# Four stretches reordered: the delta rule's next low part, GpSimd's gate products, the experts' end, the sparse attention

## The chip, the cores and the metric

One core of a Trainium2 chip runs the whole program. The metric is the device time of one execution in microseconds, the median of several runs.

## The reference

Two blocks run in a row on x of 256 x 1024 in float32. The first: a mixer with a chunked gated delta rule and an mLSTM, a cross-attention to a memory, and an expert layer (PEER), then a norm. The second: a gated feed-forward (SwiGLU), a spatial gating, a sparse attention and more SwiGLUs, each with a layer norm. What matters here, cut:

```python
# delta rule, per chunk of 64
decay = jnp.exp(jnp.where(causal, gc[..., :, None] - gc[..., None, :], -jnp.inf))
a = jnp.where(strict, jnp.einsum('nbhid,nbhjd->nbhij', kb, k) * decay, 0.0)
t_inv = lax.linalg.triangular_solve(a + eye, ...)
...
go = rmsnorm(go.transpose(0, 2, 1, 3), gdn_norm_w) * jax.nn.silu(g_z...)
...
# sparse attention: per head three softmaxes of one query
s_c = jnp.einsum('bqghd,bngd->bghqn', q_b, k_cmp) + head_bias(dist_c)   # 15 compressed keys
p_c = masked_softmax(s_c, mask_c)          # a masked entry gives 0
o_s = ... selected keys ...                # all 256 keys, causal
o_w = ... window keys ...                  # all 256 keys, causal
return g_b[..., 0:1] * o_c + g_b[..., 1:2] * o_s + g_b[..., 2:3] * o_w
...
return out @ w_o
```

## The kernel before

Every weight comes through a ring of three slots in on-chip memory (1 MB each, `Weights`, filled by SyncE's DMAs at L179 as slots are used). A float32 matrix product is made of three passes of TensorE over split operands: ScalarE writes a slot's high part in two halves of 128 x 1024 (L247, or L301 where a stage begins one slot ahead), VectorE the low part, slot minus high (L256 or L307), and TensorE multiplies high by high, high by low and low by high (L398 to L400). A slot so split is ready when VectorE has signalled `used`. The order of the work on each engine is written out by hand, and the engines meet at semaphores. A stage is a block that all five engines enter and leave together, unless stages are joined. `stand_in` (L584) issues matmuls whose result nothing reads.

- **Delta rule, `gdn_prepare` (L1250 to L1450).** The 64 x 64 triangular matrices are inverted by doubling in six levels, each in two halves of the pairs (head, tile). VectorE picks a level's entries (`pick`, L1316) and subtracts products from `inv_T` (L1336) and `inv` (L1339). TensorE makes the products (L1426, L1431, L1435), and ScalarE copies between them (L1374). Beside it the first slot of the next stage is split ahead into `x_transposed`: ScalarE the high halves at steps 3 and 5 (L1377), GpSimd the low halves (L1390).
- **Recurrences, `memory_and_recurrences` (L1453 to L1856).** TensorE mixes eight panels of the memory's keys and values (`panel(f, j)`, L398 to L400) with the chunk steps `delta(n)`, `state_product(n)` and `memory_cell(n)`. VectorE makes the panels' low parts between the steps (`low(f)`, L256). ScalarE copies the chunk results out (`delta_out(n)`, which signals `rd`). GpSimd multiplies `kw` by its weights (L1851), the gates z and mo by the head gains (L1854, L1855), and then issues the DMA that writes the position bias of 4 MB (L1856). The gates are read at the stage's end.
- **Experts' end (L2400 to L2620).** After the last expert's product of a row tile VectorE adds the tile (`add(t)`, L2602), ScalarE squares it with the sum and takes the root (L2429, L2432), VectorE scales it (`scale(t)`, L2610) and TensorE transposes tile 0 (L575), with stand-ins before and after. ScalarE (`begin.highs`, L301) and VectorE (`begin.low`, L307) split the next stage's first slot as well.
- **Sparse attention, `query_and_attend` (L3605 to L3935), then `out_and_norm` (L2763).** Eight pairs of heads. Per pair VectorE adds the bias to the scores (L3818, L3819, L3822) and takes three negated maxima (L3827, L3830, L3833), and between these does the last steps of the pair before: mask, sum, guard, reciprocal, gate, weigh (L3775 to L3802). ScalarE takes eight exponentials with a sum (L3881) and four small ones for the compressed keys (L3887), and copies the transposed probabilities of each head out in three pieces (L3897 to L3899). TensorE, in iteration n: scores of pair n, transposes of the even head of pair n-2 (`turn`, L3708 to L3712), `mix` of pair n-3 (L3726), transposes of the odd head. ScalarE's order in iteration n is below. In the last three iterations TensorE makes stand-ins. Then `out_and_norm` multiplies by w_o in four slots (24 matmuls of 128x512 each), the first split at the attention's end.

```python
            for n in range(NH // 2 + 3):
                if 2 <= n < NH // 2 + 2:
                    copy(2 * (n - 2))
                    copy(2 * (n - 2) + 1)
                if n < NH // 2:
                    exps(n)
```

## Time and profile before

| | |
|---|---|
| median of 3 runs | 2301.25 us (2296.02 to 2301.57) |
| profiled execution, its time | 2301.07 us |
| profiled execution, its span | 2299.0 us |
| granted TensorE clock, mean | 0.989 of full speed |
| TensorE busy | 2221.3 us (97%) |
| VectorE busy | 1591.0 us (69%) |
| ScalarE busy | 1176.1 us (51%) |
| GpSimd busy | 44.3 us (2%) |

The profile shows one execution. Times in it count from the span's start. Engines are PE (TensorE), PEld (its weight loads), DVE (VectorE), ACT (ScalarE), POOL (GpSimd) and SP (SyncE). L12 is line 12 of the kernel. A timeline's row has start (us), length (us), engine, line, operation and tiles. A float32 matmul outside the split products appears as two records. "[1.24 <-ACT ...]" gives the idle time before a row and what ended it. [...]

### The profile page before, as it was taken

What the parts mean: (1) busy time and instruction counts of PE and PEld (TensorE: products, weight loads), DVE (VectorE), ACT (ScalarE), POOL (GpSimd) and SP (SyncE); (2) the same over time, 40 slices, a digit from 0 to 9 for tenths busy, and PEclk for the clock granted to TensorE, in tenths of its full rate; (3) what the DMA queues carried; (4) which work ended last, traced back from release to release, by engine and by line L of the source; (5) the groups of instructions that cost most, each with busy time, mean ns of one, the idle gap of its engine ahead of it and who ended that gap; (6) DMA issues with size and microseconds to landing.
All of it is one profiled execution on the core that took longest, in us unless ns stands there. A gap on an engine that the chain in (4) does not pass through costs nothing. (4 is left out here: it accounts for less than half of the span.)

```text
span 2299.0 us, 37165 instructions
## 1 busy us (share of the span) xinstructions
PE 2221.3 (97%) x14670; PEld 1983.5 (86%) x14670; DVE 1591.0 (69%) x2807; ACT 1176.1 (51%) x2063; POOL 44.3 (2%) x23
## 2 busy tenths in 40 slices
PE   8889999999999999999999999999999999989998
PEld 8877789899999988888888889988888788868887
DVE  7866658999889976666666656766556555676555
ACT  6532444455554445565555545445443544585444
POOL 0111000100000000000000000000000000000000
PEclk9989999999999999999999999999999999999999
DMA  7407534455444446666646456545555655404552
GB/s 267 147 13 147 178 129 149 153 178 176 147 147 147 147 148 193 193 195 195 193 166 222 184 197 235 188 149 202 198 183 204 221 201 183 151 2 165 201 193 99
DMA packets 78309, 389.97 MB, mean 170 GB/s; under 512 B 9771, under 2 KB 12715, under 8 KB 49868
## 3 DMA queue, kind: packets, MB, share of 16 engines
q1 hardware_dynamic: 76684, 383.33, 47.9%
q0 software_dynamic: 1040, 4.19, 1.5%
q8 instruction: 106, 1.74, 0.3%
q10 hardware_dynamic: 432, 0.33, 0.1%
q14 instruction: 47, 0.39, 0.0%
HBM read 382.57 MB, written 5.24 MB: 169 GB/s over the span
## 5 line engine op out<-in xcount | busy, mean ns | idle before, releaser
L256 DVE TENSOR_TENSOR split_slots<-ring,split_slots 128x1024 fp32r<-128x1024 f32 x402 | 480.0, 1239 | 136.4 <-ACT split_slots L247 136.0
L247 ACT ACTIVATE split_slots<-ring 128x1024 fp32r<-128x1024 f32 x402 | 402.3, 1054 | 159.3 <-PE banks L400 138.6
L409 DVE SCALAR_TENSOR_TENSOR expert_lo<-ring,expert_hi 128x512 fp32r<-128x512 f32 x512 | 362.5, 713 | 170.6 <-ACT expert_hi L404 169.5
L3025 PE MATMUL banks<-x_transposed,split_slots 128*128 128x512 f32 x1360 | 478.3, 395 | 2.0 <-PEq L464 2.0
L404 ACT ACTIVATE expert_hi<-ring 128x512 fp32r<-128x512 f32 x512 | 323.9, 633 | 264.2 <-PE banks L400 264.2
L3026 PE MATMUL banks<-x_transposed,split_slots 128*128 128x256 f32 x1360 | 381.6, 281 | 0.0
L3025 PEld LDWEIGHTS banks<-x_transposed,split_slots 128*128 128x128 f32 x1360 | 255.4, 188 | 62.1 <-issue 2.2
L398 PE MATMUL banks<-x_transposed,expert_hi 128*128 128x256 f32 x1024 | 295.3, 288 | 6.6 <-DVE expert_lo L409 6.6
L399 PE MATMUL banks<-x_transposed,expert_hi 128*128 128x256 f32 x1024 | 289.0, 282 | 0.0
L400 PE MATMUL banks<-x_transposed,expert_lo 128*128 128x256 f32 x1024 | 289.0, 282 | 0.0
L3026 PEld LDWEIGHTS banks<-x_transposed,split_slots 128*128 128x128 f32 x1360 | 256.4, 189 | 1.5
L398 PE MATMUL banks<-expert_hi,weighted_split 128*128 128x512 f32 x512 | 200.1, 391 | 3.1 <-issue 3.1
L398 PEld LDWEIGHTS banks<-x_transposed,expert_hi 128*128 128x128 f32 x1024 | 194.5, 190 | 8.1 <-issue 4.4
L3125 DVE TENSOR_TENSOR gate_and_value<-banks,products_with_low_parts 128x512 f32<-128x512 f32 x88 | 60.8, 691 | 201.8 <-ACT products_with_low_parts L3081 201.8
L399 PE MATMUL banks<-expert_lo,weighted_split 128*128 128x512 f32 x512 | 199.8, 390 | 0.0
L400 PE MATMUL banks<-expert_hi,weighted_split 128*128 128x512 f32 x512 | 199.7, 390 | 0.0
L399 PEld LDWEIGHTS banks<-x_transposed,expert_hi 128*128 128x128 f32 x1024 | 194.4, 190 | 0.0
L400 PEld LDWEIGHTS banks<-x_transposed,expert_lo 128*128 128x128 f32 x1024 | 194.3, 190 | 0.0
L3081 ACT ACTIVATE products_with_low_parts<-banks 128x512 f32<-128x512 f32 x88 | 52.6, 597 | 245.2 <-PE banks L3026 237.4
L398 PE MATMUL banks<-x_transposed,split_slots 128*128 128x256 f32 x544 | 154.8, 285 | 2.3 <-PEq L464 2.0
L400 PE MATMUL banks<-x_transposed,split_slots 128*128 128x256 f32 x544 | 153.5, 282 | 0.0
L399 PE MATMUL banks<-x_transposed,split_slots 128*128 128x256 f32 x544 | 153.4, 282 | 0.0
(494 smaller groups left out, 4088.1 us busy)
## 6 DMA issues: line engine op xcount, KB each, us to landing
ring<-in_ffn_w SPq DMA_DIRECT2D x132, 1024.0 KB, 4.8
ring<-in_peer_u SPq DMA_DIRECT2D x128, 512.0 KB, 3.5
ring<-in_peer_v SPq DMA_DIRECT2D x128, 512.0 KB, 3.6
ring<-in_w_in SPq DMA_DIRECT2D x16, 1024.0 KB, 4.9
ring<-in_sgu_w_in SPq DMA_DIRECT2D x16, 1024.0 KB, 4.9
ring<-in_peer_wq SPq DMA_DIRECT2D x8, 1024.0 KB, 6.1
ring<-in_sgu_w_out SPq DMA_DIRECT2D x8, 1024.0 KB, 4.7
ring<-in_kv_w SPq DMA_DIRECT2D x6, 1024.0 KB, 4.8
```

The costliest lines, as they stand in the source:

```text
L247: act.activation(self.parts[:, b, 0, p], self.k.w.slot(g)[:, p], ACT.Copy).then_inc(self.high_done, 1)
L256: ins = dve.tensor_tensor(self.parts[:, b, 1, p], self.k.w.slot(g)[:, p], self.parts[:, b, 0, p].bitcast(F32), ALU.subtract)
L398: pe.matmul(out, lh, rh, start=start, stop=False)
L399: pe.matmul(out, lh, rl, start=False, stop=False)
L400: return pe.matmul(out, ll, rh, start=False, stop=stop)
L404: return act.activation(dst, src, ACT.Copy, scale=scale)
L409: return dve.scalar_tensor_tensor(dst, src, scale, hi.bitcast(F32), ALU.mult, ALU.subtract)
L3025: pe.matmul(out(j, slice(0, 2 * SEQ)), lh, k.xT.both[:, c, :, :], start=(c == 0), stop=False)
L3026: ins = pe.matmul(out(j), ll, rh, start=False, stop=(c == DC - 1))
L3081: act.activation(rest[:, n, :, :], sums(u, n, 1), ACT.Copy).then_inc(copied[n], 1)
L3125: dve.tensor_tensor(whole[:, n, :, :], sums(u, n, 0), rest[:, n, :, :], ALU.add).then_inc(joined[n], 1)
```

## The change

1. In the delta rule ScalarE makes the first high half at the stage's start and the second at step 3. VectorE makes the low halves, one before its wait for the decays and one before its wait for `w_done`. GpSimd does none of it.
2. In the recurrences GpSimd issues the bias DMA before the two gate products, and these wait for `rd` to reach 3, the third chunk's `delta_out`.
3. At the experts' end ScalarE makes each high half after the square and root of a tile, not both before; VectorE makes the first low half after `scale(0)`, not after `add(0)`.
4. In the attention the mask is a product of 16 gate columns, made once; the guard goes; the compressed scores get their negated maximum added on VectorE (`shift`), and one exponential replaces four. One copy of 128x1024 replaces three. ScalarE puts the second tile's exponentials between the two copies. The first slot of w_o is split during the attention and multiplied there: tile 0 in iteration 8, tile 1 in iteration 9, in place of the stand-ins. `out_and_norm` starts at its second slot, which is split at the attention's end.

```diff
         @block.vector
         def _(dve):
             link = linker(dve, vs)
+
+            def ahead_low(n):
+                dve.wait_ge(ahead_high, n + 1)
+                return dve.tensor_tensor(ahead_parts[1][n], ahead_slot[n], ahead_parts[0][n].bitcast(F32), ALU.subtract)
+
...
             link(dve.tensor_tensor(col[:, 3, :], s.run[:, 0, 1, :], gc, ALU.subtract))
+            ahead_low(0)
             dve.wait_ge(ps, 1)
...
+            ahead_low(1).then_inc(k.w.used[ahead % RING], 1)
             dve.wait_ge(w_done, 1)
...
+            act.wait_ge(k.w.loaded[ahead % RING], 16 * (ahead // RING + 1))
+            ahead_high_of(0)
             act.activation(col[:, 1, :], gc, ACT.Exp).then_inc(acts, 1)
...
+                if n == 3:
+                    ahead_high_of(1)
...
             k.sig.clear_other(pool)
-            for n in range(2):
-                pool.wait_ge(ahead_high, n + 1)
-                ins = pool.tensor_tensor(ahead_parts[1][n], ahead_slot[n], ahead_parts[0][n].bitcast(F32), ALU.subtract)
-            ins.then_inc(k.w.used[ahead % RING], 1)
...
+            pool.dma_start(k.a["bias_rows"].rearrange("p h x -> h p x"),
+                           bias.rows[:, :].unsqueeze(1).broadcast_to([NH, P, DISTS])).then_inc(k.bias_stored, 16)
             pool.wait_ge(landed, 32)
+            pool.wait_ge(rd, 3)
...
             act.wait_ge(w_low, KEYS)
-            begin.highs(act)
...
+                begin.high(act, t)
...
             add(0)
-            begin.low(dve, 0)
             add(1)
             dve.wait_ge(gain_landed, 16)
             scale(0)
+            begin.low(dve, 0)
             scale(1)
...
+        def output_product(pe, i):
+
+            if i == 0:
+                pe.wait_ge(biased, 3 * NH // 2)
+                pe.wait_ge(written, 2)
+                rows.ready(pe, 0)
+            wh, wl = rows.rows(0)
+            for r in range(2):
+                ins = down_tile(pe, k, k.xT.at(slice(0, P), r), (wh[:, r, :], wl[:, r, :]), i, r == 0, False)
+            if i == 1:
+                ins.then_inc(rows.eaten, 1)
...
                 if n == NH // 2:
-                    pe.wait_ge(biased, 3 * NH // 2)
-                    stand_in(pe, k, 6)
-                if n == NH // 2 + 1:
-                    stand_in(pe, k, 4)
-                    pe.wait_ge(expd, NH // 2)
-                    stand_in(pe, k, 12)
+                    output_product(pe, 0)
...
+                if n == NH // 2 + 1:
+                    output_product(pe, 1)
+                if n == NH // 2 + 2:
+                    mix(pe, n - 3)
...
+                    if n == 2:
+                        rows.low(dve, 0)
...
+            rows.low(dve, 1)
             for j in range(NH // 2 - 3, NH // 2):
                 output(j)
...
+        def mask_gates(dve):
+
+            own = gates[:, :, :].rearrange("p i (h n) -> p i h n", n=3)[:, 0, :, 0]
+            dve.wait_ge(narrow_read, 2)
+            dve.tensor_tensor(own, own, masks[:, 0, 0:1].broadcast_to([P, NH]), ALU.mult).then_inc(gates_masked, 1)
...
+        def shift(dve, q):
             own = cs[q % 3][:, :, :, 0:NCMP]
+            dve.wait_ge(negmax, 3 * q + 3)
+            dve.tensor_tensor(own, own, spread(c[q % 3][:, 0, :, :, 0], NCMP), ALU.add).then_inc(shifted, 1)
...
+            def cmp_exps(q):
+                own = cs[q % 3][:, :, :, 0:NCMP]
+                act.wait_ge(shifted, q + 1)
+                act.activation(own, own, ACT.Exp).then_inc(expd, 1)
...
-                act.activation(pT[b][:, :, :, :].rearrange("p a i n -> p (a i n)"), k.psum[:, 4, :], ACT.Copy).then_inc(copied, 1)
-                act.activation(flat(pT_last[b][:, :, :]), k.psum[:, 5, 0:B], ACT.Copy).then_inc(copied, 1)
-                act.activation(cT[b][0:NCMP, :], k.psum[0:NCMP, 5, B:2 * B], ACT.Copy).then_inc(copied, 1)
+                act.activation(turned_T[b][:, :, :].rearrange("p a n -> p (a n)"),
+                               k.psum[:, 4:6, :].rearrange("p b n -> p (b n)"), ACT.Copy).then_inc(copied, 1)
...
                 if 2 <= n < NH // 2 + 2:
                     copy(2 * (n - 2))
+                if n < NH // 2:
+                    exps(n, 1)
+                if 2 <= n < NH // 2 + 2:
                     copy(2 * (n - 2) + 1)
                 if n < NH // 2:
-                    exps(n)
+                    exps(n, 0)
+                    cmp_exps(n)
```

VectorE's instructions at the start of the delta rule, before:

```order
L1297 TENSOR_TENSOR gc_diagonal<-constants_sb,running_logs 128x512
L1299 COPY gdn_columns<-beta 128x8
L1301 TENSOR_TENSOR gdn_columns<-running_logs 128x8
L1303 TENSOR_TENSOR decay_up<-banks,running_logs 128x512
L1304 SCALAR_TENSOR_TENSOR decay_low<-decay_up,constants_sb 128x512
```

and now:

```order
L1302 TENSOR_TENSOR gc_diagonal<-constants_sb,running_logs 128x512
L1304 COPY gdn_columns<-beta 128x8
L1306 TENSOR_TENSOR gdn_columns<-running_logs 128x8
L1300 TENSOR_TENSOR x_transposed<-ring,x_transposed 128x4x256
L1309 TENSOR_TENSOR decay_up<-banks,running_logs 128x512
L1310 SCALAR_TENSOR_TENSOR decay_low<-decay_up,constants_sb 128x512
```

The first low half stands ahead of `decay_up`, for which VectorE waits on TensorE.

ScalarE's instructions of one pair in the middle of the attention, before:

```order
L3897 ACTIVATE probabilities_T<-banks 128x512
L3898 ACTIVATE probabilities_last_T<-banks 128x256
L3899 ACTIVATE cmp_probabilities_T<-banks 15x256
L3881 ACTIVATE scores_second,softmax_columns<-scores_second,softmax_columns 128x256 x4
L3881 ACTIVATE scores_first,softmax_columns<-scores_first,softmax_columns 128x128 x4
L3887 ACTIVATE cmp_scores<-cmp_scores,softmax_columns 128x15 x4
L404 ACTIVATE x_transposed<-banks 128x256
```

(the three copies stand there twice, for the even and the odd head), and now:

```order
L3917 ACTIVATE probabilities_T<-banks 128x1024
L3903 ACTIVATE scores_second,softmax_columns<-scores_second,softmax_columns 128x256 x4
L3917 ACTIVATE probabilities_T<-banks 128x1024
L3903 ACTIVATE scores_first,softmax_columns<-scores_first,softmax_columns 128x128 x4
L3910 ACTIVATE cmp_scores<-cmp_scores 128x4x15
L404 ACTIVATE x_transposed<-banks 128x256
```

The larger exponentials stand between the two heads' copies.

VectorE at the experts' end, now (before, the first L307 row stood between the two adds):

```order
L2610 TENSOR_TENSOR x_natural<-banks,x_natural 128x1024 x2
L2614 RECIPROCAL final_stats<-final_stats 128x1
L2618 SCALAR_TENSOR_TENSOR x_natural<-x_natural,final_stats,final_gain 128x512 x2
L307 TENSOR_TENSOR split_slots<-ring,split_slots 128x1024
L2614 RECIPROCAL final_stats<-final_stats 128x1
L2618 SCALAR_TENSOR_TENSOR x_natural<-x_natural,final_stats,final_gain 128x512 x2
L307 TENSOR_TENSOR split_slots<-ring,split_slots 128x1024
```

Both adds stand together, and each scaling is followed by a low half.

## Rows read from the trace of the kernel before

**Rows 1.** VectorE, delta rule: timeline; L1316's own (ns min/median/max).
```profile
134.88 0.69 DVE L1303 TENSOR_TENSOR decay_up<-banks,running_logs 128x512 f32<-128x512 f32 x1 [1.48 <-PE banks L1396]
...
L1316 DVE TENSOR_TENSOR A_level<-A,constants_sb x12: 411/418/2471, 138.3 to 157.5; 128x256 f32<-128x256 f32 x12
...
147.81 2.47 DVE L1316 TENSOR_TENSOR A_level<-A,constants_sb 128x256 f32<-128x256 f32 x1
...
165.39 1.22 DVE L1352 COPY w_T<-banks 128x1024 f32<-128x1024 f32 x1 [1.39 <-PE banks L1446]
```

**Rows 2.** Timeline of GpSimd, delta rule and recurrences.
```profile
147.66 2.34 POOL L1390 TENSOR_TENSOR x_transposed<-ring,x_transposed 128x1024 fp32r<-128x1024 f32 x1 [0.71 <-ACT x_transposed L1377]
...
188.49 3.33 POOL L1855 TENSOR_TENSOR mlstm_o<-mlstm_o,head_gains 128x1024 f32<-128x1024 f32 x1
```

**Rows 3.** Timeline of TensorE, delta rule.
```profile
142.80 0.66 PE L1431 MATMUL banks<-AtW,inv 64*64 64x64 f32 x16
...
151.09 1.12 PE L1426 MATMUL banks<-inv_T,A_level 64*64 64x64 f32 x16 [2.37 <-DVE inv L1339]
...
156.00 0.66 PE L1431 MATMUL banks<-AtW,inv 64*64 64x64 f32 x16
...
159.22 1.35 PE L1431 MATMUL banks<-AtW,inv 64*64 64x64 f32 x32
```

**Rows 4.** Timelines of VectorE and TensorE, recurrences.
```profile
186.24 6.66 DVE L256 TENSOR_TENSOR split_slots<-ring,split_slots 128x1024 fp32r<-128x1024 f32 x2
...
193.04 0.55 PE L398 MATMUL banks<-memory_T,split_slots 128*128 128x256 f32 x1 [2.85 <-DVE split_slots L256]
```

**Rows 5.** Windows: stretch, length, busy us (instructions) of PE to POOL, clock, DMA.
```profile
167.00:171.00 4.00, 4.00 (x21) 4.00 (x22) 1.87 (x4) 1.91 (x2) 1.41 (x2) 0.57 0.18 51
...
193.00:198.10 5.10, 5.06 (x24) 5.09 (x24) 4.95 (x6) 1.22 (x2) 0.00 (x0) 0.50 0.85 92
...
2044.00:2062.00 18.00, 13.37 (x133) 10.39 (x132) 15.26 (x35) 15.51 (x64) 0.00 (x0) 1.00 0.01 1
```

**Rows 6.** Timelines of ScalarE, TensorE and VectorE, experts' end.
```profile
1197.38 2.01 ACT L301 ACTIVATE split_slots<-ring 128x1024 fp32r<-128x1024 f32 x2 [5.27 <-DMA ring<-in_ffn_w]
...
1196.50 0.40 PE L400 MATMUL banks<-expert_hi,weighted_split 128*128 128x512 f32 x1
...
1202.58 1.42 DVE L2610 SCALAR_TENSOR_TENSOR x_natural<-x_natural,final_stats,final_gain 128x512 f32<-128x512 f32 x2
...
1203.91 1.22 DVE L307 TENSOR_TENSOR split_slots<-ring,split_slots 128x1024 fp32r<-128x1024 f32 x1
...
1206.65 1.07 PE L575 MATMUL banks<-ident,x_natural 128*128 128x128 f32 x8 [0.30 <-PEq L479]
```

**Rows 7.** Timelines, attention; the last row groups lines by form.
```profile
1998.42 1.23 DVE L3818 TENSOR_TENSOR scores_second<-banks,position_bias 128x1024 f32<-128x1024 f32 x1 [1.29 <-PE banks L3696]
...
2045.55 1.21 DVE L3818 TENSOR_TENSOR scores_second<-banks,position_bias 128x1024 f32<-128x1024 f32 x1
...
2047.69 0.88 ACT L3887 ACTIVATE cmp_scores<-cmp_scores,softmax_columns 128x15 f32<-128x15 f32 x4
...
2048.61 0.22 DVE L3775 TENSOR_TENSOR cmp_scores<-cmp_scores,cmp_masks 128x60 f32<-128x60 f32 x1 [1.04 <-ACT cmp_scores L3887]
...
2051.09 0.60 ACT L3897 ACTIVATE probabilities_T<-banks 128x512 f32<-128x512 f32 x1 [1.25 <-PE banks L3712]
...
2053.46 1.21 DVE L3818 TENSOR_TENSOR scores_second<-banks,position_bias 128x1024 f32<-128x1024 f32 x1
...
2066.74 3.74 PE L584 MATMUL banks<-ones,ident 128*128 128x128 f32 x32
...
2078.74 0.50 PE L398 MATMUL banks<-split_slots,x_transposed 128*128 128x512 f32 x1
...
L3881 ACT ACTIVATE scores_second<-scores_second,softmax_columns 128x256 f32<-128x256 f32 x32 | 15.8, 494 | 6.3 <-DVE softmax_columns L3827 6.3
```

**Rows 8.** Windows, the attention's output stage, columns as in rows 5.
```profile
2079.00:2101.00 22.00, 22.00 (x95) 17.66 (x95) 14.03 (x16) 11.22 (x14) 0.00 (x0) 1.00 0.36 143
```

110 lines of the change are left out of this document (48 added, 62 removed).

## The prediction

> **What bounds the kernel.** I read the page first: TensorE is busy 97% of the span, so time can only leave where TensorE waits, works for nothing, or runs at the lower clock. So I read the four changed stretches one by one: timelines of VectorE, GpSimd and TensorE, then windows for the granted clock.
>
> In the delta rule's inversion VectorE's 12 picks (L1316) take 0.418 us in the median, but one takes 2.47 [rows 1]. It lies under a GpSimd subtraction that runs from 147.66 to 150.00 [rows 2]. TensorE then idles 2.37 us, and its next group takes 1.12 where a group takes 0.66 [rows 3]. In the recurrences two halves of a low part take 6.66 us together [rows 4] where one alone takes 1.22 [rows 6]; they end 1.08 us after the GpSimd product that starts at 188.49 and takes 3.33 [rows 2]. [...] At the experts' end ScalarE waits 5.27 us for a weight slot before it may square the rows [rows 6]. In the attention a pair of heads takes 7.91 us (2045.55 to 2053.46), of which VectorE idles 1.04 for ScalarE's small exponentials and ScalarE idles 1.25 between its two copies for TensorE's transposes [rows 7]. So the pairs are paced by ScalarE's 6.66 us plus one uncovered wait.
>
> **The sum, part by part** (against the profiled execution's 2301.07 us; the median of the runs, 2301.25, is the same for this purpose).
>
> *A. Delta rule: 3.5 us gained.* An undisturbed level takes 159.22 - 156.00 = 3.22 us. From 142.80 four levels would end at 155.68, not 159.22 [rows 3]: 3.54. Added to VectorE are two halves of 1.22 [rows 6]. The first falls into an idle of 1.48 us before L1303, the second into one of 1.39 before L1352 [rows 1]; I cost both at nothing. With that cover gone they would cost up to 2.4, so A lies between 1.1 and 3.9. ScalarE's first half, about 1.0 us (half of L301's 2.01 [rows 6]), now stands before its exponentials; VectorE's wait for them comes later, and if it did not hide, it would cost that 1.0, which the lower bound covers.
>
> What the row shows is a two-operand VectorE operation held until GpSimd's is over. [...]
>
> *B. Recurrences: 5.3 us gained.* Gone are the wait of 2.85 [rows 4] and the half clock behind it: 5.10 us at 0.50 would be 2.55 [rows 5]. I take 2.85 + 2.5. The two products (3.33 for the longer [rows 2]) now start after the third chunk's delta has been read. There they run beside the low part of panel 5. They can hold it 2 to 3.3 us, but TensorE has another panel and a chunk to do before it needs that part; I cost it at nothing, and at 3.3 at worst. The bias DMA now stands ahead of the products on GpSimd's queue. It starts some 6 us sooner and could slow a weight load. A panel's slot is asked for two panels before its use, so that too is nothing. B is 2 to 5.4.
>
> *C. Experts' end: 1.2 us gained.* ScalarE now squares tile 0 before it waits for the slot. The last product starts at 1196.50 and takes 0.40 [rows 6]. From 1197.0 VectorE is then busy without a break: the add of tile 1 (as long as a half, 1.14 to the next start), two scalings of 1.55 (the 1.42 pair and its reciprocal), two low halves of 1.14 and 1.22 [rows 6]. That ends at 1203.6. Now the stage ends when TensorE's stand-ins do, 0.30 before 1206.65 [rows 6], so 2.75 is won. But TensorE would be done near 1202.3 and idle 1.6 us before the next stage. At the block start at 167 such an idle is followed by 4.00 us at 0.57 [rows 5], a loss of 1.7. I take 1.5 off; the ends are 0 and 2.75.
>
> *D. Attention: 13.4 us gained*, in three terms.
> D1, the pairs. VectorE's own work is 7.91 - 1.04 = 6.87 a pair [rows 7]. The mask and guard go (some 0.2 of issue), the shift comes (0.15): 6.8. ScalarE's falls from 6.66 to about 6.1, since four small exponentials (0.88 [rows 7]) become one (0.3), and its idle of 1.25 is now filled by four exponentials of 0.49 [rows 7]. VectorE becomes the pace. Seven steps lead from pair 0 (1998.42) to pair 7 (2053.46): 55.04 us [rows 7]. After: the first stays at the mean 7.9 (it waits for the gate columns), six take 6.8, one of them carries the two halves of row 0's low part (2.3), and one waits about 0.5 for the last query products: 51.5. D1 = 3.5, between 0 (ScalarE still paces) and 5.
> D2, the tail from pair 7's start to the end of the last mix, now 2078.74 - 2053.46 = 25.3, with 32 stand-in passes of 3.74 us in it that delay a transpose [rows 7]. After, I walk the chain, with pieces of the same work as in rows 7 or estimated from it: pair 7's adds and first maximum 3.2; the second half's exponentials 2.0; the copy between 1.0; the first half's 1.55; the one small one 0.3; sum, reciprocal, gate and weighing 2.8; a wait for the copy of head 13, 1.1; transposes, mix and copy of head 14, 3.2; head 15's transposes 0.9; half of the moved product 2.8; the last mix 2.1. That is 21.0: D2 = 4.3, between 2 and 5.5.
> D3, the moved product: 24 of the output's 96 matmuls, 22.00 us for 95 recorded [rows 8], 0.232 each, leave the output stage: 5.6. Their first half falls where TensorE waited for VectorE, the second is counted in D2. Behind them the next slot must be split in time: row slot 2 is ready some 5.0 us after the last mix (ScalarE's last output and two halves, then VectorE's two) and wanted 5.6 after it, when slot 1's 24 matmuls are done. A miss costs under 1.
>
> Together 3.5 + 5.3 + 1.2 + 13.4 = 23.4, and 2301.07 - 23.4 = **2277.7 us**.
>
> [...] In the rows the clock stays at 1.00 from 2044 to 2062, where TensorE is busy only 13.37 of 18 us [rows 5], and the new tail is denser. [...]
>
> **The rivals.**
> R1, ScalarE still paces the pairs (a 128x1024 copy dearer than the three it replaces, or the copies still found waiting): D1 is 0, D2 halves to 2.1, the gain 17.7, so 2283.4. For it: ScalarE ends the waits today. Against: its work falls below VectorE's. Chance 0.12.
> R2, the clock falls in the attention's tail: the 8.7 us of TensorE's work from head 14's transposes to the last mix take twice as long: gain 23.4 - 8.7 = 14.7, so 2286.4. Chance 0.07.
> R3, the change only moves the hold: VectorE's stalls were hidden or come back at another step, and A and B are nothing: 23.4 - 8.8 = 14.6 is left, 2286.5. The waits in rows 3 and 4 speak against it. Chance 0.05.
> R4, slower. In the new order ScalarE's copy of an odd head stands behind exponentials that wait for VectorE's maximum of a later pair, which waits for TensorE's scores, which stand behind transposes that wait for such a copy. Round the ring: 3.2 + 2.0 + 1.0 + 0.9 + 2.1 + 0.9 + 1.9 and 0.4 of waits = 12.4 us. As I read the order it closes only after two pairs, 6.2 a pair, under the 6.8. If it closed in one, seven steps would take 86.8 instead of 55.0: 31.8 lost against 23.4 - 3.5 = 19.9 won elsewhere, 2313.0. It decides the sign from 10.7 us a pair. Chance 0.03.
> The forecast has 0.73.
>
> **How the numbers follow.** 2277.7 is the likeliest case. All parts at their best give 3.9 + 5.4 + 2.75 + 16.1 = 28.2, 2273; with a microsecond of spread between executions on either side of that and of R1 the range is 2272 to 2285; what lies above is R2, R3 and R4, 0.15, and some of R1's spread. About 0.3%, 6.9 us, is what a measurement of this kernel can tell. Everything but R4 is faster by more: 0.95; within 0.3% I leave 0.02 for losses that add up; slower 0.03.
>
> **What would show it.** A: no pick over 0.5 us, levels 3.2 apart. B: the low part of panel 2 in 2.4 us, TensorE's wait gone, clock 1.00 behind it; a held L256 near panel 5 with nobody waiting. C: squares right after the first add, the stage ended by VectorE, a low clock at the next start. D: pairs 6.8 apart, VectorE without idle, no wait between ScalarE's copies, the last mix some 8 us sooner. Pairs at 7.9 would make D1 wrong, a clock under 1.00 in the tail D2, an idle before row slot 2 D3.

## The result and the profile after

The changed kernel takes 2271.39 us in the median of 4 runs (2269.86 to 2275.18), the kernel before 2300.57 (2296.02 to 2301.57): ratio 0.9886, 95% interval 0.9872 to 0.9900. That is 29.2 us, more than the forecast's 23.4, and the median lies 0.6 us below the range's low end. The profiled execution took 2271.95 us, its span is 2269.8.

Both kernels were timed twice more. The medians differ by 25.5 us (2298.21 and 2272.69) and by 26.0 (2298.39 and 2272.36). So some 26 us is the change, and the rest of the first 29 is the scatter of single executions. Where the gain stands in the two profiles is found by pairing the same instruction in both traces and watching how far apart its two starts are:

| stretch | change's part | forecast | seen |
|---|---|---|---|
| start to the delta rule (code unchanged) | none | 0 | 4.4 |
| delta rule | A | 3.5 | 3.6 |
| recurrences | B | 5.3 | 5.3 |
| cross-attention to the experts' last product (unchanged) | none | 0 | 1.3 |
| experts' end | C | 1.2 | 2.9 |
| SwiGLU to the attention (unchanged) | none | 0 | -2.1 |
| attention and its output | D | 13.4 | 14.0 |

The parts sum to 25.7, the unchanged stretches to 3.6 (sums of unrounded figures). The -2.1 is mostly clock too: the changed kernel's profile has a granted clock of 0.80 over 1529 to 1536, where the same work ran at 1.00 before, and 1.5 us are lost there.

**The unchanged start.** TensorE's first products in the timelines, of the kernel before and then of the changed one (start, length):

```profile
20.57 0.40 PE L359 MATMUL banks<-x_transposed,split_slots 128*128 128x256 f32 x1
20.78 0.30 PE L356 MATMUL banks<-x_transposed,split_slots 128*128 128x256 f32 x1
```

```profile
14.69 0.39 PE L356 MATMUL banks<-x_transposed,split_slots 128*128 128x256 f32 x1 [2.32 <-DVE split_slots L307]
14.92 0.28 PE L359 MATMUL banks<-x_transposed,split_slots 128*128 128x256 f32 x1
15.04 0.28 PE L356 MATMUL banks<-x_transposed,split_slots 128*128 128x256 f32 x1
```

The same matmul starts 0.21 us apart at first and 0.12 later, the spacings that these 128x256 products have elsewhere at a granted clock of 0.50 (24 in 5.10 us [rows 5]) and of 1.00 (0.12 apart from 1190.80 on in the changed kernel). Before, the higher level came at 20.8, in the changed kernel's profile at 14.9; it is read from the spacing alone, since the windows show 1.00 over 13 to 21 in both profiles. That is worth 2.7 us by 43. The other 1.7 come in the window 60 to 90, where the granted clock is 0.94 before and 1.00 in the changed kernel. In the 14 profiles of this case (all have this stretch unchanged up to the first mixer panels) the first rise came between 14.8 and 20.8. The start of the delta rule (the product `gc_diagonal`) lies at 132.31 before and at 127.89 after, and in the eleven others that leave all ahead of it alone between 127.85 and 132.11. An early rise alone does not give an early start: in e6 it came at 14.9, but the clock was low again later (products 0.21 us apart from 15.9 to 19.1, 0.94 over 60 to 90), and the delta rule began at 131.05. So the 4.4 us are the placing of the low clock, not the change.

**A and B.** The picks in the changed kernel (the tile's own view: count, ns min/median/max, first and last start), then the timelines of VectorE and GpSimd in the recurrences:

```profile
L1322 DVE TENSOR_TENSOR A_level<-A,constants_sb x12: 417/420/425, 133.9 to 149.5; 128x256 f32<-128x256 f32 x12
```

```profile
178.26 2.35 DVE L256 TENSOR_TENSOR split_slots<-ring,split_slots 128x1024 fp32r<-128x1024 f32 x2
...
204.26 2.92 DVE L256 TENSOR_TENSOR split_slots<-ring,split_slots 128x1024 fp32r<-128x1024 f32 x2
207.11 0.68 DVE L1647 TENSOR_TENSOR mlstm_state<-mlstm_state,chunk_decays 128x516 f32<-128x516 f32 x1
210.53 0.69 DVE L1682 TENSOR_TENSOR mlstm_state<-mlstm_state,banks 128x516 f32<-128x516 f32 x1 [2.74 <-PE banks L1595]
...
200.24 2.38 POOL L1864 TENSOR_TENSOR gdn_z<-gdn_z,head_gains 128x1024 f32<-128x1024 f32 x1 [21.28 <-ACT convolved_T L1789]
202.59 2.37 POOL L1865 TENSOR_TENSOR mlstm_o<-mlstm_o,head_gains 128x1024 f32<-128x1024 f32 x1
```

No pick is over 0.43 us [rows 1 had 2.47]. In the kernel before a second pick was held as well, and behind both TensorE ran at half clock (timeline of VectorE, then window):

```profile
145.31 1.92 DVE L1316 TENSOR_TENSOR A_level<-A,constants_sb 128x256 f32<-128x256 f32 x1
```

```profile
150.00:154.00 4.00, 2.92 (x56) 2.94 (x58) 1.75 (x6) 0.38 (x1) 0.00 (x0) 0.57 0.01 4
```

By the paired starts 2.3 of A's 3.6 us are the two holds and 1.2 the half clock behind them.

In the recurrences the picture is as forecast. The low part of panel 2 takes 2.35 us [rows 4 had 6.66], and TensorE has no wait for it. The products now hold a low part for 0.57 us (2.92 against 2.35), and VectorE then waits 2.74 us for TensorE anyway. The window behind it, 168 to 245, has the clock at 1.00:

```profile
168.00:245.00 77.00, 74.93 (x549) 62.15 (x548) 46.81 (x74) 28.87 (x47) 8.05 (x4) 1.00 0.72 160
```

**C.** ScalarE, then TensorE at the experts' end (timelines):

```profile
1180.99 1.06 ACT L2436 ACTIVATE expert_weights<-x_natural 128x1024 f32<-128x1024 f32 x1 [3.41 <-DVE x_natural L2610]
...
1182.85 1.06 ACT L301 ACTIVATE split_slots<-ring 128x1024 fp32r<-128x1024 f32 x1 [0.38 <-DMA ring<-in_ffn_w]
```

```profile
1189.26 1.06 PE L575 MATMUL banks<-ident,x_natural 128*128 128x128 f32 x8 [1.56 <-PEq L479]
```

The square follows the first add, the slot is hardly waited for [rows 6 had 5.27], and TensorE idles 1.56 us ahead of the next stage, as forecast. The window behind it, however, has the clock at 1.00:

```profile
1189.83:1193.83 4.00, 3.75 (x32) 3.51 (x31) 3.65 (x6) 3.82 (x5) 0.00 (x0) 1.00 0.90 266
```

The kernel before had a half clock inside this stage, which the forecast did not name. TensorE there waited 2.29 us for tile 0, and its transposes and stand-ins then ran slowly (timeline, window); in the changed kernel the same eight transposes start without a wait and take 1.04 us:

```profile
1201.87 1.97 PE L575 MATMUL banks<-ident,x_natural 128*128 128x128 f32 x8 [2.29 <-DVE x_natural L2610]
```

```profile
1201.90:1205.90 4.00, 4.00 (x22) 4.00 (x23) 3.19 (x5) 1.61 (x5) 0.00 (x0) 0.58 0.02 8
```

So part of C's 2.9 us is this half clock: some 1.2, by an estimate from when VectorE (1203.91 + 1.22) and when the stand-ins ended [rows 6].

**D.** Timelines of VectorE (pairs 6 and 7), ScalarE and TensorE (tail), and the window of the tail:

```profile
2027.87 1.22 DVE L3839 TENSOR_TENSOR scores_second<-banks,position_bias 128x1024 f32<-128x1024 f32 x1
...
2034.33 1.22 DVE L3839 TENSOR_TENSOR scores_second<-banks,position_bias 128x1024 f32<-128x1024 f32 x1
...
2037.53 0.51 ACT L3903 ACTIVATE scores_second<-scores_second,softmax_columns 128x256 f32<-128x256 f32 x1 [0.62 <-DVE softmax_columns L3847]
...
2046.22 0.30 PE L3717 MATMUL banks<-ident,scores_first 128*128 128x128 f32 x1 [1.21 <-ACT probabilities_T L3917]
...
2055.11 0.50 PE L398 MATMUL banks<-split_slots,x_transposed 128*128 128x512 f32 x1
```

```profile
2034.00:2056.00 22.00, 20.60 (x156) 14.71 (x157) 13.28 (x29) 14.93 (x41) 0.00 (x0) 1.00 0.14 48
```

Pair 0 starts at 1983.16. The seven steps take 7.76, 7.73, 8.41, 6.13, 8.20, 6.48 and 6.46: 51.17 us, against 55.04 [rows 7]. Before they took 8.26, 7.22, 8.08, 6.47, 8.67, 8.43 and 7.91, so 3.4 of the 3.9 us were won in the last two steps and 0.5 in the first five. The tail (pair 7's start to the first matmul behind the last mix) is 2055.11 - 2034.33 = 20.78, against 25.28 [rows 7, 8]. In the last two steps ScalarE waits 0.62 us a pair for VectorE's maximum, and VectorE waits for nobody; in the second and the fifth VectorE still waits for TensorE's scores, 0.90 and 1.65 us. The first product of slot 1 comes in the row at 2055.11, the one of slot 0 is done.

### The profile page after: what moved, and what is told of

It is laid out like the page before. It is cut to its first block and busy times, and to the rows that moved or that the text cites. A ratio compares the mean times of both kernels' runs of the same rounds, so it can differ in the third digit from the quotient of the medians.

```text
span 2269.8 us, 36975 instructions
## 1 busy us (share of the span) xinstructions
PE 2204.5 (97%) x14606; PEld 1967.8 (87%) x14606; DVE 1584.4 (70%) x2802; ACT 1169.8 (52%) x2007; POOL 38.2 (2%) x21
```

## The experiments

All are edits of the changed kernel. Each stage is read by itself, from a mark on its start to a mark on its end, which takes the low clock elsewhere out. Where a variant ran once its total says little, since that moves by 5 to 7 us between executions of one kernel. No run undoes what went from VectorE's own work in the attention (mask and guard): that part stands in all of them.

**e1_two_inputs**

```diff
             k.sig.clear_other(pool)
+            for n in range(2):
+                pool.wait_ge(Ys, 4 + n)
+                pool.tensor_tensor(scrap[:, n, :], ahead_slot[n], ahead_parts[0][0].bitcast(F32), ALU.subtract)
...
             pool.wait_ge(landed, 32)
-            pool.wait_ge(rd, 3)
...
             act.wait_ge(w_low, KEYS)
+            begin.highs(act)
...
-                begin.high(act, t)
```

> Three edits to the changed kernel, in stages that don't touch each other, each read in its own stage. (1) Delta rule: VectorE makes the low halves as changed, and GpSimd makes two subtractions with two inputs in on-chip memory into an unused tile, 128x1024 each, at the levels where it made its halves. Main theory (a running GpSimd operation holds VectorE): picks of over 2 us come back and the inversion is 2 to 4.5 us longer, though none of that work is needed. Rival (what was gained came from moving ScalarE's first high half or from the shorter queue): no pick over 0.5 us, levels stay 3.22 us apart. (2) Recurrences: the wait for the third chunk's delta is taken away, the bias DMA stays first. Main theory (it is the products' place): the low part of panel 2 is held again, over 5 us instead of 2.35, TensorE waits about 2.9 us and the stage is about 5.3 us longer. Rival (the DMA's place made the gain): the stage is unchanged. (3) Experts' end: ScalarE makes both high halves before it squares the first tile, VectorE as changed. Main theory: the whole 2.85 us of this part are lost, with ScalarE waiting for the weight slot before the square. Rival (VectorE's order made the gain): at most 1.2 us lost. The whole run, if the main theories hold: 2271.4 + 3.5 + 5.3 + 2.85 = about 2283.

Measured: 2279.65 us. The picks (the tile's own view), then, in the timelines, GpSimd's subtractions, the low part of panel 2 and TensorE behind it:

```profile
L1323 DVE TENSOR_TENSOR A_level<-A,constants_sb x12: 410/418/1974, 133.9 to 151.4; 128x256 f32<-128x256 f32 x12
```

```profile
142.34 4.97 POOL L1402 TENSOR_TENSOR scrap<-ring,x_transposed 128x1024 f32<-128x1024 f32 x2 [36.13 <-ACT AtW L1387]
...
178.55 7.60 DVE L256 TENSOR_TENSOR split_slots<-ring,split_slots 128x1024 fp32r<-128x1024 f32 x2
...
186.29 0.55 PE L398 MATMUL banks<-memory_T,split_slots 128*128 128x256 f32 x1 [3.78 <-DVE split_slots L256]
```

Two picks are held (1.88 and 1.97 us) and the inversion is 1.9 us longer, a little below the bound of 2. That is the holds alone: TensorE idles 1.67 us behind them, not 2.37, and the clock stays at 1.00 (145.84 to 149.84), so the 1.2 us of half clock in A do not come back here. (1.5 of the 1.9 us are regained in the next block, which ran at 1.00 in e1 and, over 159 to 162.4, at 0.60 in the changed kernel.) The low part takes 7.60 us and the recurrences are 5.7 us longer, against 5.3. At the experts' end the next stage's first gate product comes 20.27 us after the first add, against 17.52: 2.75 lost. So the place of the products makes B and ScalarE's order is enough to undo C.

**e2_one_input**

```diff
             k.sig.clear_other(pool)
+            for n in range(2):
+                pool.wait_ge(Ys, 4 + n)
+                pool.tensor_scalar(scrap[:, n, :], ahead_slot[n], 1.0, None, ALU.mult)
...
-            pool.dma_start(k.a["bias_rows"].rearrange("p h x -> h p x"),
-                           bias.rows[:, :].unsqueeze(1).broadcast_to([NH, P, DISTS])).then_inc(k.bias_stored, 16)
             pool.wait_ge(landed, 32)
             pool.wait_ge(rd, 3)
...
+            pool.dma_start(k.a["bias_rows"].rearrange("p h x -> h p x"),
+                           bias.rows[:, :].unsqueeze(1).broadcast_to([NH, P, DISTS])).then_inc(k.bias_stored, 16)
...
             add(0)
+            begin.low(dve, 0)
             add(1)
             dve.wait_ge(gain_landed, 16)
             scale(0)
-            begin.low(dve, 0)
```

> Three edits to the changed kernel, each read in its own stage. (1) Delta rule: as in e1_two_inputs, but GpSimd's two unneeded operations are multiplications by a constant, with one input in on-chip memory. If only two-input operations of GpSimd hold VectorE: no held pick, levels 3.22 us apart. If any operation of GpSimd that reads on-chip memory does: held picks as in e1_two_inputs. (2) Recurrences: the wait for the third chunk's delta stays, the bias DMA goes back behind the two products. Main theory: nothing changes, the stage is within 0.3 us. Rival (the DMA's place counts): up to 5 us. (3) Experts' end: ScalarE as changed, VectorE makes the first low half between the two adds, as before. By the chain, low half 0 then waits for the high half behind tile 0's root, and the second add behind that: the stage is about 1.5 us longer. Rival (VectorE's order is indifferent): 0. The whole run by the main theories: 2271.4 + 3 + 0 + 1.5 = about 2276.

Measured: 2289.58 us, 18 above the changed kernel, where 5 were expected. The picks; then the timelines of GpSimd, TensorE (recurrences' end) and VectorE (experts' end); then the bias transfer in the view of the DMA issues (its last number is us from issue to landing):

```profile
L1323 DVE TENSOR_TENSOR A_level<-A,constants_sb x12: 410/418/507, 138.2 to 153.8; 128x256 f32<-128x256 f32 x12
```

```profile
146.52 5.50 POOL L1402 TENSOR_SCALAR scrap<-ring 128x1024 f32<-128x1024 f32 x2 [36.01 <-ACT AtW L1387]
...
209.21 1.23 POOL L1868 DMA_DIRECT2D bias_rows<-bias_by_distance  x1
...
257.27 3.65 PE L1910 MATMUL banks<-ident,convolved_T 128*128 128x128 f32 x16 [12.29 <-PEq L479]
...
1201.35 1.23 DVE L307 TENSOR_TENSOR split_slots<-ring,split_slots 128x1024 fp32r<-128x1024 f32 x1 [2.90 <-ACT split_slots L301]
```

```profile
bias_rows<-bias_by_distance POOLq DMA_DIRECT2D x1, 4096.0 KB, 47.6
```

(1) GpSimd's operations with one input run beside four picks, and the longest of these is 0.51 us: no hold, and the inversion is as long as in the changed kernel. (2) Both theories fall. The bias transfer takes 47.6 us from its issue to its landing, 209.21 + 47.6 = 256.8, and the stage's SyncE waits for it: TensorE idles 12.29 us and the stage is 11.4 longer. In the kernel before the same order did no harm, since the DMA left near 192. Delaying the products makes it necessary to put the DMA first. (3) VectorE waits 2.90 us for the high half, and the second add comes 5.28 us behind the first instead of 2.73: 2.65 us lost (20.17 against 17.52), not 1.5. Both halves of C are needed.

**e3_copies_together**

```diff
                     copy(2 * (n - 2))
-                if n < NH // 2:
-                    exps(n, 1)
-                if 2 <= n < NH // 2 + 2:
                     copy(2 * (n - 2) + 1)
                 if n < NH // 2:
+                    exps(n, 1)
                     exps(n, 0)
...
-            stand_in(pe, k, 12, 7)
             turn_chunks(pe, k, k.x[:, 0, :], 0, banks, 4, normed)
-            stand_in(pe, k, 8, 7)
```

> Two edits to the changed kernel. (1) Attention: ScalarE makes the copies of both heads one behind the other and then all eight exponentials, as before; one large copy, one small exponential and the product in the tail stay as changed. Main theory (what D1 gained is ScalarE's wait of 1.25 us between the copies, now filled): its work of about 6.1 us and the wait make 7.35 us a pair against 6.46 now, so that the seven steps take about 55 us against 51.17, with ScalarE waiting between the copies and VectorE idle each pair. Rival (the fewer instructions alone made the gain): the seven steps stay at 51 to 52 us. (2) Experts' end: the 20 stand-in matmuls are left out. They are nobody's input. If the clock at the next stage's start hangs on them, the granted clock there is near 0.5 for some 4 us and the next stage begins with matmuls of twice the length, 1.5 to 2 us lost; if not, nothing changes. In the profile of the changed kernel the clock was 1.00 there with them.

Measured: 2276.97 us. ScalarE waits 1.25 us between the copies again:

```profile
2035.96 1.02 ACT L3915 ACTIVATE probabilities_T<-banks 128x1024 f32<-128x1024 f32 x1 [1.25 <-PE banks L3719]
```

But only the last two steps are longer (7.08 and 7.09); the other five are as in the changed kernel, so the seven take 52.41, not 55. The tail takes 22.34, 1.56 more. Neither theory had this: the early steps are set by other things than ScalarE. Without stand-ins at the experts' end TensorE idles 2.95 us ahead of the next stage, whose first 4 us (1189.87 to 1193.87) run at 0.50, and 2.4 us are lost.

**e4_three_pieces** and **e6_small_exponentials**

```diff
-                act.activation(turned_T[b][:, :, :].rearrange("p a n -> p (a n)"),
-                               k.psum[:, 4:6, :].rearrange("p b n -> p (b n)"), ACT.Copy).then_inc(copied, 1)
+                act.activation(pT[b][:, :, :].rearrange("p a n -> p (a n)"), k.psum[:, 4, :], ACT.Copy)
+                act.activation(pT_last[b][:, :, :].rearrange("p a n -> p (a n)"), k.psum[:, 5, 0:B], ACT.Copy)
+                act.activation(cT[b][0:NCMP, :, :].rearrange("p a n -> p (a n)"), k.psum[0:NCMP, 5, B:2 * B], ACT.Copy).then_inc(copied, 1)
```

> Attention: the copy of 128x1024 in three pieces again (512, 256 and 256 columns, the last of 15 rows), all else as changed. Main theory (VectorE paces the pairs, ScalarE has 0.62 us to spare in each): three pieces take 1.02 us to the next start where the one takes 0.90, so 0.24 us a pair go into ScalarE's spare time and the seven steps stay within 0.3 us of 51.17. Rival (ScalarE's work paces): 0.24 us a pair, up to 1.7 us. In the tail, where a copy is on the path at three heads, 0.2 to 0.4 us.

```diff
-                act.wait_ge(shifted, q + 1)
-                act.activation(own, own, ACT.Exp).then_inc(expd, 1)
+                act.wait_ge(negmax, 3 * q + 3)
+                for hh in range(2):
+                    for i in range(TILES):
+                        own = cs[q % 3][:, hh, i, 0:NCMP]
+                        ins = act.activation(own, own, ACT.Exp, bias=c[q % 3][:, 0, hh, i, 0:1])
+                ins.then_inc(expd, 1)
```

> Attention: the compressed scores get four small exponentials with a bias on ScalarE again (0.88 us) in place of VectorE's shift and one exponential (0.24), all else as changed. Main theory: with 0.62 us to spare in a pair ScalarE is at its limit, the pairs 5 to 7 take 6.5 to 6.8 us instead of 6.46 and the seven steps 51.2 to 52.5; VectorE's sum waits for them as before. In e3_copies_together the order alone was worth 0.62 us in each of the last two pairs; before against e3 the instructions were worth 0.83 a pair, and this run shows how much of that is the small exponentials: all of it if they are on the path, none if the pieces of the copy and VectorE's own steps make it.

Measured: e4 2274.23 us, steps 51.26, tail 21.06; e6 2274.35 us, steps 51.15, tail 21.24. In the steps neither costs anything: ScalarE's 0.62 us to spare takes it. In the tail, which is a chain, they cost 0.28 and 0.46.

The profile of e4 also has the experts' end as in the changed kernel, and there the clock does fall. Window of the 4 us from tile 1's transposes on, as shown of the changed kernel above:

```profile
1191.79:1195.79 4.00, 4.00 (x21) 3.76 (x22) 3.36 (x5) 2.99 (x4) 0.00 (x0) 0.57 0.72 238
```

The gate product comes 19.32 us after the first add, not 17.52: 1.8 lost. But 0.7 of that was lost ahead of the first product of the next stage, for the idle was longer here, 2.22 us and not 1.56: ScalarE waited 1.91 us for the weight slot, and 0.38 in the changed kernel's profile. ScalarE and TensorE in e4:

```profile
1186.26 1.06 ACT L301 ACTIVATE split_slots<-ring 128x1024 fp32r<-128x1024 f32 x1 [1.91 <-DMA ring<-in_ffn_w]
...
1191.79 1.48 PE L575 MATMUL banks<-ident,x_natural 128*128 128x128 f32 x8 [2.22 <-PEq L479]
```

**e7_order_alone** (both edits above at once)

> Attention: ScalarE's three pieces of the copy and its four small exponentials, both as before, in the changed order (the second tile's exponentials between the copies); the product in the tail as changed. Each of the two edits by itself left the steps at 51.2 (51.26 and 51.15). Together ScalarE's work in a late pair is its 5.84 (6.46 less the 0.62 it waits) + 0.64 + 0.24 = 6.72 us, more than VectorE's 6.46. If order and fewer instructions are two ways to the same slack: pairs 5 to 7 take 6.5 to 6.75 us and the seven steps 51.3 to 52, so the order alone gives nearly all of D1. If the small edits add up with the order: 52.5 or more.

Measured: 2275.34 us, steps 51.32, tail 21.64. The last step takes 6.53 us. With the order changed and ScalarE's instructions as before, 3.7 of the steps' 3.9 us are there; with the shorter instructions and the old order (e3) it was 2.6. They don't add, since each does away with the same wait. Neither is the order or the instructions quite alone: VectorE's shorter work is in both, and before it had 6.87 us of it a pair where the late pairs now take 6.46. What that part is worth by itself is not shown.

**e5_product_late** and **e8_late_with_stand_ins**

```diff
                 if n == NH // 2:
-                    output_product(pe, 0)
...
                 if n == NH // 2 + 1:
+                    output_product(pe, 0)
                     output_product(pe, 1)
```

> Attention: both halves of the moved product stand behind head 15's transposes, none ahead of head 12's; no stand-ins. Main theory (the first half fills a wait of TensorE for VectorE, the second delays the last mix): the tail from pair 7 to the first matmul behind the last mix grows from 20.78 by 2.8 us to about 23.6, the seven steps stay at 51.17. Rival (the first half too delays head 12's transposes): the tail grows by less than 2. For the clock (the rival by which it falls in the tail): TensorE now idles some 2.5 us ahead of head 12's transposes with neither product nor stand-ins; if the clock falls there, the tail grows by up to 5 us more.

e8 has the same, and ahead of head 12's transposes

```diff
+                    pe.wait_ge(biased, 3 * NH // 2)
+                    stand_in(pe, k, 20)
```

> Attention: as e5_product_late (the whole moved product behind head 15's transposes), but 20 stand-in matmuls stand ahead of head 12's transposes, where e5 left TensorE idle for 2.34 us and then ran at a clock of 0.50 to 0.53 for some 7 us. Theory (e5's 5.54 us are 2.8 for the product and 2.7 for the clock): the clock stays at 1.00 and the tail is 23.6 us. Rival (the second half of e5's loss is the order of the product, not the clock): the tail stays at 26.3.

Measured: e5 2276.25 us, tail 26.32. TensorE and the window of e5:

```profile
2039.37 0.45 PE L3717 MATMUL banks<-ident,scores_first 128*128 128x128 f32 x1 [2.34 <-DVE scores_second L3822]
```

```profile
2039.00:2046.00 7.00, 6.63 (x34) 4.34 (x35) 3.50 (x9) 3.19 (x12) 0.00 (x0) 0.52 0.00 0
```

The tail grew by 5.54, and for 7 us the clock was 0.52. e8 took 2280.27 us, its tail 25.26, between the two theories. I had sized its stand-ins by the recorded matmul, and one is two of them:

```profile
2042.03 4.63 PE L584 MATMUL banks<-ones,ident 128*128 128x128 f32 x40
```

At 4.63 us they outlast the wait, and head 12's transposes come 1.7 us later behind pair 7 than in the changed kernel. The clock is 1.00 over 2036 to 2060, and 25.26 - 1.7 is the 23.6 expected. So e5's 5.5 us are 2.8 for the product and about 2.7 for the clock. The traces show the second figure directly too: head 14's transposes, ahead of which e5 has neither half of the product, start 14.63 us after pair 7 in e5 and 11.89 in the changed kernel. Nor is the first half quite free where it now stands: head 12's transposes start 6.60 us after pair 7 with it and 6.32 in e5 without it.

**after_again** and **after_third**, the changed kernel itself.

> The changed kernel itself, to see how far its runs and those of the kernel before scatter and where the clock is low in another profile of it. If what was won beyond 23.4 us is chance (the clock at the very start, 4.4 us in the two profiles, and in later stages), the runs of both kernels spread over 3 to 6 us, and the difference of many runs lies near the sum of the parts as the stages show them, 3.6 + 5.3 + 2.9 + 14.0 = 25.8, less about 1 for the clock behind the experts' end. If the change itself has a part that I don't see, the difference stays at 29.

> The changed kernel once more, beside best2 and the same runs of the kernel before. As in after_again: a median near 2272.5, 25 to 27 us below that of the kernel before, if 25.8 less the clock is the whole of what the change is worth.

Measured: 2272.69 us (2270.94 to 2275.32, ratio 0.9887, 0.9871 to 0.9904) and 2272.36 (2269.62 to 2275.12, ratio 0.9885, 0.9869 to 0.9902). The median of all its 12 runs is 2272.0, that of 21 runs of the kernel before, 2294.93 to 2301.67, is 2298.4: 26.4 apart.

**best1** and **best2**, versions beyond the change. In the changed kernel's profile GpSimd, VectorE and TensorE in the experts' choice:

```profile
404.74 2.34 POOL L2452 TENSOR_TENSOR position_hits<-position_hits,top_keys 128x1024 f32<-128x1024 f32 x1 [11.88 <-DVE position_hits L2515]
...
404.97 2.65 DVE L409 SCALAR_TENSOR_TENSOR expert_lo<-ring,expert_hi 128x512 fp32r<-128x512 f32 x1
...
407.77 0.36 PE L398 MATMUL banks<-x_transposed,expert_hi 128*128 128x256 f32 x1 [3.74 <-DVE expert_lo L409]
```

The low half takes 2.65 us instead of 0.69 beside GpSimd's product of 2.34: the same hold as in rows 1 and 2, at a place that the change left alone. In the mixer a GpSimd operation with one input does slow VectorE, unlike in e2. The two timelines of the changed kernel, then VectorE's of best2, where the two no longer meet:

```profile
102.66 3.56 POOL L1145 TENSOR_SCALAR convolved_T<-convolved_T 128x1024 f32<-128x1024 f32 x1 [40.61 <-ACT convolved_T L1080]
...
102.36 3.19 DVE L256 TENSOR_TENSOR split_slots<-ring,split_slots 128x1024 fp32r<-128x1024 f32 x2
```

```profile
109.55 2.35 DVE L256 TENSOR_TENSOR split_slots<-ring,split_slots 128x1024 fp32r<-128x1024 f32 x2
```

The two subtractions take 3.19 us instead of 2.35, and GpSimd's operation 3.56 instead of the 2.78 that it takes in best2.

In best1 and best2 the product of the hits for heads 2 to 7 is VectorE's (`choose`), and a quarter of the moved product stands behind head 13's transposes:

```diff
-            for h in range(PEER_HEADS):
+            for h in range(FILL_FROM):
                 pool.wait_ge(hits, h + 1)
...
                 if h >= 1:
+                    choose(h - 1)
                     reduce(h - 1)
...
+                if n == NH // 2:
+                    output_product(pe, 1, (0,))
                 if n == NH // 2 + 1:
-                    output_product(pe, 1)
+                    output_product(pe, 1, (1,))
```

In best1 alone the low halves of row slot 0 move behind pair 4:

```diff
-                    if n == 2:
+                    if n == 4:
                         rows.low(dve, 0)
```

In best2 alone the mixer's last low part comes behind a normalisation, and low halves of the expert tiles come sooner:

```diff
-                if m + BUFFERS < MIXER_PANELS:
+                if m + BUFFERS < MIXER_PANELS - 1:
                     split.low(dve, m + BUFFERS)
...
                     normalise(KEYS_FIRST[m - 11])
+                if m == MIXER_PANELS - 1 - BUFFERS:
+                    split.low(dve, m + BUFFERS)
...
-                most = 0 if h < FILL_FROM else 4 + per_head * (h - FILL_FROM)
+                most = 0 if h < FILL_FROM else max(6, 4 + per_head * (h - FILL_FROM))
...
-                    elif h > FILL_FROM or pauses[0] > 10:
+                    elif h > FILL_FROM or pauses[0] > 9:
```

> Three further edits to the changed kernel. (1) Experts' choice: GpSimd's product of the hits for heads 2 to 7 goes to VectorE, 1.22 us each. In the profile of the changed kernel a low half of an expert tile is held 2.65 us instead of 0.69 under that product, and TensorE waits 3.74 us for the low half behind it, then 4 us run at a clock of 0.61. If the hold is what makes the wait, TensorE's wait goes below 2 us and 2 to 4 us are won; if VectorE's own load makes it, the wait stays and the added 1.22 us a head cost up to 1 us. (2) Attention: the low halves of row slot 0 are made after pair 4, where VectorE waits 1.65 us for scores, not after pair 2: 0 to 1.65 us won in the steps (51.17 now). (3) A quarter of the moved product stands between the transposes of head 13 and 14, where TensorE waits 1.21 us: the tail 1.2 us shorter (20.78 now). Together 2271.4 - 2.5 - 1.2 - 1.2, some 2266, range 2263 to 2270.

Measured: 2270.38 us (2267.66 to 2271.57), ratio to the kernel before 0.9872 (0.9855 to 0.9888), 2.3 under the changed kernel timed beside it, and short of the forecast (2266, range 2263 to 2270). TensorE's wait fell from 3.74 to 1.77 us. By the pairing with the changed kernel's trace 2.9 us are won by 433, with the clock behind the wait, and 2.4 are left at the end of the choice; the tail is 19.39. The low halves behind pair 4 won nothing (steps 51.29): the third step is 0.42 shorter, the fifth 0.54 longer. So 2.35 us of work cost the third step only 0.42; without it VectorE waits there 1.76 us for scores.

> The changed kernel with four further edits. (1) GpSimd's product of the hits for heads 2 to 7 on VectorE, as in best1 (TensorE's wait 3.74 to 1.77 us there, about 2.6 us won). (2) Two more low halves of the expert tiles made within head 2's choice, and the first one a pause earlier: TensorE's waits of 1.56 and 1.77 us there become shorter, 1 to 3 us won. (3) A quarter of the moved product between the transposes of heads 13 and 14, as in best1: 1.4 us. (4) Mixer: the last panel's low part (3.19 us with its hold by a GpSimd scaling) is made behind the second normalisation, not ahead of it; TensorE waits 3.61 us for that normalisation and does not need the low part before its transposes are over: 2 to 3 us won, and perhaps the half clock behind the wait. Together 7 to 9 us under the changed kernel in the same call, some 2264.

Measured: **2262.63 us** (2261.36 to 2264.36), ratio 0.9847 (0.9834 to 0.9861), 9.7 under the changed kernel timed beside it (forecast 7 to 9). TensorE in best2's timeline, at the mixer's transposes and in the experts' choice:

```profile
109.69 1.09 PE L1029 MATMUL banks<-ident,convolved_T 128*128 128x128 f32 x8 [0.55 <-DVE convolved_T L1183]
...
395.16 0.39 PE L398 MATMUL banks<-x_transposed,expert_hi 128*128 128x256 f32 x1 [0.75 <-DVE expert_lo L409]
...
403.43 0.36 PE L398 MATMUL banks<-x_transposed,expert_hi 128*128 128x256 f32 x1 [0.92 <-DVE expert_lo L409]
```

The waits were 3.61, 1.58 and 3.74 us. By the pairing with the changed kernel's trace 5.8 us are won in the mixer (3.1 are the wait, the rest is mostly the clock, 1.00 behind the transposes where it was 0.57 over 108 to 116), 4.7 in the experts' choice by 408, with the clock behind it, of which 4.0 are left at its end, and 1.4 in the tail.

## Why the prediction was right, and where its sum was off

- **A** held: 3.6 for 3.5. The halves on VectorE cost nothing: the first is followed by an idle of 0.19 us, the second by 0.25, what is left of the 1.48 and 1.39 in [rows 1]. That a running two-input GpSimd operation holds a VectorE pick is shown by e1: two picks of 1.88 and 1.97 us instead of 0.42, and 1.9 us of the 3.6 come back. I had read one held pick; there were two, and 1.2 of the 3.6 us are the half clock behind them. The forecast took the whole time between levels, so the sum holds these terms without naming them. How far the hold reaches is shown for single pairs of operations only: e2 has none beside a one-input multiplication (no pick over 0.51 us), the mixer a slowing beside another one (3.19 us instead of 2.35).
- **B** held: 5.3, and 5.7 when undone in e1. The moved products do hold a low part, by 0.57 us, and nobody waits, as priced. What I priced at nothing and understood wrongly was the bias DMA. I asked what it would slow by leaving sooner; e2 shows that it had to leave sooner, or the stage would have ended 11.4 us later.
- **C** was the mis-sized term: 2.9 for 1.2. The mechanism was right (square after the first add, stage ended by VectorE, 1.56 us of idle). The step that failed is "I take 1.5 off" for the half clock. In ten profiles that have this stage as changed, eight show no loss (17.5 us to the gate product). Best1 shows it, 1.5 behind the same 1.56 us of idle, with the clock at 0.68 over the 4 us from tile 1's transposes on (1188.86 to 1192.86); e4 loses 1.8, but behind 2.22 us of idle, and 0.7 of it is a weight slot that landed late. It was right as a possibility, and wrong as the likeliest case. And the 2.75 that I ascribed to VectorE's shorter chain holds some 1.2 us of half clock in the kernel before, which I had not seen.
- **D** held as a sum, 14.0 for 13.4, by terms 3.9 (3.5), 4.5 (4.3) and 5.6 (5.6). That D1 fits is partly luck. I had every step but the first fall to 6.8; instead the first five together gain only 0.5, since there VectorE also waits for TensorE's scores (0.90 and 1.65 us, where I had put 0.5 once), and the last two gain 3.4, to 6.46. The two low halves, which I priced at 2.3 us, cost 0.42 by best1.
- **The rivals.** R1 is excluded: ScalarE waits, also with three pieces (e4) or small exponentials (e6). R3 is excluded by the table, R4 by the steps. R2 did not happen, but e5 shows that the clock can fall in this tail: TensorE was left idle for 2.34 us ahead of head 12's transposes, the clock was 0.52 over the 7 us from there on, and this cost 2.7 us, not the 8.7 that I priced. In the changed kernel, with real work in the stand-ins' place, it stayed at 1.00 over 2034 to 2056, and in e8, with stand-ins there, over 2036 to 2060.
- **The range.** Its low end, 2272, took all parts at their best but only one microsecond of spread. The two kernels' runs spread over 5 to 7 us, so the difference of two medians of four is itself loose by some 3. The first measurement was 29.2, the three together some 26. What stays open is why the clock's rise at the start comes now at 14.9 and now at 20.8, and why the same 1.56 us of idle let the clock fall in one of nine profiles; no run here varied that.

## What to carry to other kernels

Here a GpSimd operation with two inputs was paid for by a two-input VectorE operation beside it (a pick of 2.47 us instead of 0.42, two halves of a low part in 6.66 us instead of 2.35), and one with a single input was in the mixer (3.19 us instead of 2.35) but not in e2 (at most 0.51): look for VectorE rows several times their median, see whether TensorE waits behind them, and move the work either to VectorE itself or to where VectorE waits anyway. When you delay work on a queue, ask first what stands behind it, above all a long transfer whose landing somebody waits for (47.6 us in e2, whose stage became 11.4 longer). Two cures for the same wait did not add (3.7 and 2.6 us alone, 3.9 together): price them together, against the engine that paces next, and compare stages between marks, not totals, when a few microseconds are at stake.

## What the runs showed of the hardware

- Beside GpSimd's two-input subtractions (128x1024, 2.34 to 2.5 us) two-input picks of VectorE took 1.88 to 2.47 us instead of 0.42; beside its one-input multiplication of the same size (two in 5.50 us) at most 0.51. Beside another one-input multiplication, in the mixer, two 128x1024 subtractions took 3.19 us instead of 2.35, and the multiplication 3.56 instead of 2.78.
- The clock's rise at the program's start, by the spacing of the products (0.21 us, then 0.12), moved by 6 us between profiles of the same code. Behind 1.56 us of idle at the experts' end (1.55 in e7) the clock fell in one of nine (best1, 0.68 over 4 us); behind 1.59 at the recurrences' start it fell in the kernel before (0.57) and in the changed one (0.60) and stayed at 1.00 in e1. Elsewhere it fell, among others, behind idles of 2.22 (e4, 0.57), 2.29 and 2.37 (the kernel before, 0.58 and 0.57), 2.34 (e5, 0.52) and 2.85 us (the kernel before, 0.50), and stayed at 1.00 behind 1.67 (e1, delta rule) and behind 2.42 (the changed kernel, at 78.7). No length of idle that parts the two is shown.
- A 4 MB transfer issued by GpSimd took 47.3 to 48.2 us from its issue to its landing in the 14 profiles, whether it left between 174 and 182, at 192 or at 209.
